# Last feed-forward stage: seven block products on token halves in place of eight

## What is computed

```python
D_FF_2 = -(-8 * D_MODEL // (3 * 256)) * 256          # 2816
...
h2 = modulate_2(x, shift2, scale2)                   # (1, 512, 1024)
y = (silu(h2 @ w_gate) * (h2 @ w_up)) @ w_down       # 2816 hidden columns
x = layer_norm(ALPHA * x + gate2 * y, ln2_g, ln2_b)
```

## Time and profile before

| | |
|---|---|
| median of 3 runs | 1970.53 us (1969.19 to 1971.74) |
| span of the profiled execution | 1965.3 us |
| median less span | 5.2 us |
| busy: PE, DVE, ACT, POOL | 97%, 60%, 40%, 17% of the span |
| last stage, first matmul to the norm's end | about 1582 to 1965 us |

### The profile page before, as it was taken

One profiled execution on the slowest core, in us unless ns is written; L12 is line 12 of the kernel. 1 busy time (PEld: TensorE's weight loads), 2 busy tenths in 40 slices (PEclk: granted clock), 3 DMA queues, 4 the chain that ended last, 5 costly groups with the idle time before them and its releaser, 6 DMA issues.

```text
span 1965.3 us, 22312 instructions
## 1 busy us (share of the span) xinstructions
PE 1906.1 (97%) x8952; PEld 1577.2 (80%) x8952; DVE 1180.5 (60%) x1853; ACT 779.4 (40%) x1180; POOL 343.6 (17%) x307
## 2 busy tenths in 40 slices
PE   4999999999999999999999999999999999999997
PEld 3788888878888887888788888877898778888886
DVE  6687665576676745665655644476777754433446
ACT  4677622352223235222422222256677442222223
POOL 4323111021111112002300000036533130000003
PEclk9999999999999999999999999999999999999998
DMA  9522366266566434432545432313211223223221
GB/s 333 150 84 70 134 223 237 88 226 221 217 209 219 150 107 158 164 127 86 213 173 192 173 127 86 108 65 129 70 44 65 88 85 100 93 90 103 95 99 43
DMA packets 126232, 267.54 MB, mean 136 GB/s; under 512 B 4576, under 2 KB 33264, under 8 KB 126129
## 3 DMA queue, kind: packets, MB, share of 16 engines
q1 hardware_dynamic: 121168, 248.59, 37.0%
q0 software_dynamic: 4960, 17.53, 2.5%
HBM read 261.84 MB, written 8.45 MB: 138 GB/s over the span
## 4 chain that ended last, share of the span: by engine, by line
PE 70%; DVE 3%; ACT 2%; POOL 2%; issue 1%; DVEq 0%; POOLq 0%; ACTq 0%
PE ps L624 22%; PE ps L626 22%; PE ps L625 22%; PE ps L784 1%; PE ps L773 0%; ACT t L1212 0%; PE ps L762 0%; ACT t L1216 0%; POOL t L2316 0%; PE ps L801 0%; PE ps L802 0%; PE ps L800 0%; DVE t L1628 0%; DVE t L1613 0%; POOL t L2125 0%
## 5 line engine op out<-in xcount | busy, mean ns | idle before, releaser
L624 PE MATMUL ps<-t 128*128 128x512 f32 (+1 forms) x2504 | 966.7, 386 | 10.3 <-POOL t L2220 4.2
L626 PE MATMUL ps<-t 128*128 128x512 f32 (+1 forms) x2504 | 958.9, 383 | 0.0
L625 PE MATMUL ps<-t 128*128 128x512 f32 (+1 forms) x2504 | 955.0, 381 | 0.0
L1549 DVE TENSOR_TENSOR t<-t 128x2048 fp32r<-128x2048 f32 x133 | 305.4, 2296 | 440.4 <-ACT t L1163 440.2
L624 PEld LDWEIGHTS ps<-t 128*128 128x128 f32 x2504 | 470.7, 188 | 104.5 <-POOL t L2125 5.6
L626 PEld LDWEIGHTS ps<-t 128*128 128x128 f32 x2504 | 470.3, 188 | 96.4
L625 PEld LDWEIGHTS ps<-t 128*128 128x128 f32 x2504 | 470.5, 188 | 90.8 <-issue 1.0
L1163 ACT ACTIVATE t<-t 128x2048 fp32r<-128x2048 f32 x133 | 254.3, 1912 | 612.8 <-PE ps L626 605.3
L1613 DVE SCALAR_TENSOR_TENSOR t<-ps,t 128x512 f32<-128x512 f32 x184 | 131.7, 748 | 81.4 <-PE ps L626 78.0
L1561 DVE CUSTOM_DVE_ANT_0 t<-t 128x1024 f32<-128x1024 f32 x144 | 174.8, 1255 | 6.7 <-DMA t<-in_adakv_t 3.5
L2125 POOL TENSOR_TENSOR t<-t 128x512 fp32r<-128x512 f32 x88 | 115.5, 1332 | 196.8 <-ACT t L1170 196.2
(11 more groups left out here) (171 smaller groups left out, 1526.1 us busy)
## 6 DMA issues: line engine op xcount, KB each, us to landing
t<-in_ada SPq DMA_DIRECT2D x48, 1024.0 KB, 5.9
t<-in_gate SPq DMA_DIRECT2D x22, 1024.0 KB, 5.1
t<-in_up SPq DMA_DIRECT2D x22, 1024.0 KB, 5.1
t<-in_down SPq DMA_DIRECT2D x22, 1024.0 KB, 5.0
t<-in_w_in SPq DMA_DIRECT2D x17, 1024.0 KB, 5.7
t<-in_w_mlp_in SPq DMA_DIRECT2D x16, 1024.0 KB, 5.3
t<-in_w_mlp_out SPq DMA_DIRECT2D x16, 1024.0 KB, 5.0
t<-in_ada_t POOLq DMA_DIRECT2D x13, 1024.0 KB, 6.0
```

The lines of the kernel that those rows point to most:

```text
L624: pe.matmul(o, wh, xh, start=first, stop=False)
L625: pe.matmul(o, wh, xl, start=False, stop=False)
L626: return pe.matmul(o, wl, xh, start=False, stop=last)
L1549: dve.tensor_tensor(WL[:, n % NW, :], raw[:, n % NRAW, :], WH[:, n % NW, :].bitcast(F), ALU.subtract).then_inc(w_lo_d.sem, w_lo_d.up("slot ...
```

## The change

Eighteen gate and up blocks of 1024 rows by 256 columns (shape "S", like B) are multiplied by a form of Strassen's scheme. The block is cut in quarters (row halves, column halves of 128), the input in quarters (feature halves, token halves of 256). Seven products of a quarter or a sum of quarters with an input quarter or a sum of them replace the eight; each is 4 `mm3` with 256 token columns, 12 matmuls, 84 in a block in place of 48 with 512 columns. The plain form stays for chunk 0 (gate and up) and for all of down.

The sums of weight quarters are made by POOL (`weight_sums`, four instructions a block, into the `csb` buffers), split by ACT (`sums_hi`) and DVE (`sums_lo`) into `SS`. Of the raw weights only three quarters are split (`raw_hi`, `raw_lo`). The four sums of input quarters are made and split once, during chunk 0, into `TT`, from an unsplit copy of the input `h6_all` that the norm before now keeps whole. The products lie in half banks of PSUM; ACT copies the first one out, DVE joins them in four steps (`first` to `fourth`). Then Silu (`silu`), the product with the gate (`times_gate`) and the split of the hidden tile (`hidden_hi`, `hidden_lo`) work on 1024 elements at once. The hidden tile has one buffer in place of two. A raw buffer is loaded again only when POOL has summed it too. Down of chunk 5 now goes "k" in its first half, as the other chunks did before.

```diff
-plan_ffn2(1)
...
+def plan_last():
+
+    for f in range(4):
+        for w, what in (("gate1", "gate"), ("up1", "up")):
+            for p in range(2):
+                if f:
+                    plan_role("S", w, 0, 512 * f + 256 * p, what, f, p)
+                else:
+                    plan_role("A", w, 512 * p, 0, what, f, p)
+        for hf in range(2):
+            plan_role("A", "down1", 512 * f, 512 * hf, "down", f, hf)
+    plan_role("S", "gate1", 0, 2560, "gate", 4, 0)
+    plan_role("S", "up1", 0, 2560, "up", 4, 0)
+    plan_role("S", "gate1", 0, 2048, "gate", 5, 0)
+    plan_role("C", "down1", 2560, 0, "down4", 4, 0)
+    plan_role("S", "gate1", 0, 2304, "gate", 5, 1)
+    for p in range(2):
+        plan_role("S", "up1", 0, 2048 + 256 * p, "up", 5, p)
+    for hf in range(2):
+        plan_role("A", "down1", 2048, 512 * hf, "down", 5, hf)
...
+            def seven_products(w, c0, before_last=None):
+                n = take("S", w, 0, c0)
+                b = bank_set(n)
+                hi, lo = slot_view(WH, n), slot_view(WL, n)
+                tops = [(HH[0][:, k, 0:256], HH[1][:, k, 0:256]) for k in range(KT)]
+                ends_ = [(HH[0][:, k, 256:512], HH[1][:, k, 256:512]) for k in range(KT)]
+                turned = [[(TT[:, 0, i, k, :], TT[:, 1, i, k, :]) for k in range(4)] for i in range(4)]
+                plain = [[(hi[:, k, blocks[m]], lo[:, k, blocks[m]]) for k in range(KT)] for m in range(2)]
+                sums = [[(SS[:, 0, i, blocks[k]], SS[:, 1, i, blocks[k]]) for k in range(4)] for i in range(4)]
+
+                def product(at, weights, inputs, name):
+                    o = region(b, at)
+                    for k in range(4):
+                        (wh, wl), (xh, xl) = weights[k], inputs[k]
+                        ins = mm3(o, wh, wl, xh, xl, k == 0, k == 3)
+                    ins.then_inc(mm.sem, mm.up("product", n, name))
+
+                on.wait_ge(w_lo_d, "raw", n, 0)
+                claim(4 * b)
+                product(0, plain[0][0:4], tops[0:4], 1)
+                product(1, plain[0][4:8], tops[4:8], 2)
+                on.wait_ge(w_lo_d, "raw", n, 1)
+                on.wait_ge(d_turn, "lo", 3)
+                claim(4 * b + 1)
+                product(3, plain[1][4:8], turned[3], 4)
+                mm.also("raw used", n)
+                on.wait_ge(d_sums, "pair", n, 0)
+                claim(4 * b + 2)
+                product(5, sums[0], turned[0], 5)
+                product(2, sums[1], turned[1], 6)
+                if before_last:
+                    before_last()
+                on.wait_ge(d_sums, "pair", n, 1)
+                product(4, sums[2], turned[2], 7)
+                claim(4 * b + 3)
+                product(6, sums[3], ends_[4:8], 3)
+                mm.also("slot", n)
+                freed[4 * b] = [(d_join, ("first", n))]
+                freed[4 * b + 1] = freed[4 * b + 2] = [(d_join, ("third", n))]
+                freed[4 * b + 3] = [(d_join, ("fourth", n))]
...
+                    for w in ("gate1", "up1"):
+                        for p in range(2):
+                            seven_products(w, 512 * f + 256 * p)
+                    down(f, "ki")
+                seven_products("gate1", 2560)
+                seven_products("up1", 2560)
+                seven_products("gate1", 2048)
...
+                def raw_hi(n, part):
+                    on.wait_ge(raw_in[n % NRAW], "landed", n)
+                    on.wait_ge(mm, "raw used" if in_products(n - NW) else "slot", n - NW)
+                    act.activation(raw_part(WH, n, part), raw_part(raw, n, part), ACT.Copy).then_inc(
+                        w_hi.sem, w_hi.up("raw", n, part))
+                def sums_hi(n, pair):
+                    on.wait_ge(p_sums, "pair", n, pair)
+                    if BEFORE[n] is None:
+                        on.wait_ge(d_turn, "lo", 3)
+                    else:
+                        on.wait_ge(mm, "product", BEFORE[n], (6, 3)[pair])
+                    act.activation(sum_pair(0, pair), csb[pair][:, :], ACT.Copy).then_inc(
+                        a_sums.sem, a_sums.up("pair", n, pair))
...
+                def hidden_hi(n):
+                    f, p = ROLE[n][1:]
+                    on.wait_ge(d_evac, "times", n)
+                    on.wait_ge(mm, "used", "act2", 1, f - 1)
+                    act.activation(AC7[:, 0, 2 * p:2 * p + 2, :].rearrange("p a n -> p (a n)"), joined(n), ACT.Copy).then_inc(
+                        a_hi.sem, a_hi.up("act2", 1, f, p))
...
+                def raw_lo(n, part):
+                    on.wait_ge(w_hi, "raw", n, part)
+                    dve.tensor_tensor(raw_part(WL, n, part), raw_part(raw, n, part), raw_part(WH, n, part).bitcast(F),
+                                      ALU.subtract).then_inc(w_lo_d.sem, w_lo_d.up("raw", n, part))
+                    if part:
+                        w_lo_d.also("slot", n)
+
+                def sums_lo(n, pair):
+                    on.wait_ge(a_sums, "pair", n, pair)
+                    dve.tensor_tensor(sum_pair(1, pair), csb[pair][:, :], sum_pair(0, pair).bitcast(F), ALU.subtract).then_inc(
+                        d_sums.sem, d_sums.up("pair", n, pair))
+
+                def first(n):
+                    on.wait_ge(a_evac, "first product", n)
+                    on.wait_ge(mm, "product", n, 6)
+                    f, p = ROLE[n][1:]
+                    if ROLE[n][0] == "up" and f > 1:
+                        on.wait_ge(a_hi, "act2", 1, *((f - 1, p) if (f, p) != (5, 1) else (3, 1)))
+                    elif ROLE[n][0] == "up":
+                        on.wait_ge(a_hi, "act2", 1, 0, 2 * p + 1)
+                    dve.tensor_tensor(joined(n)[:, 0:512].rearrange("p (a n) -> p a n", a=2), doubled(p1_b[:, :]),
+                                      two_regions(bank_set(n), 1, 2), ALU.add).then_inc(d_join.sem, d_join.up("first", n))
+
+                def second(n):
+                    on.wait_ge(mm, "product", n, 7)
+                    on.wait_ge(d_join, "first", n)
+                    dve.tensor_tensor(u34_b[:, :].rearrange("p (a n) -> p a n", a=2), doubled(joined(n)[:, 256:512]),
+                                      two_regions(bank_set(n), 4, 5), ALU.add).then_inc(d_join.sem, d_join.up("second", n))
+
+                def third(n):
+                    on.wait_ge(d_join, "second", n)
+                    dve.tensor_tensor(joined(n)[:, 512:1024].rearrange("p (a n) -> p a n", a=2), doubled(u34_b[:, 0:256]),
+                                      two_regions(bank_set(n), 3, 5), ALU.add).then_inc(d_join.sem, d_join.up("third", n))
+
+                def fourth(n):
+                    on.wait_ge(mm, "product", n, 3)
+                    dve.tensor_tensor(joined(n)[:, 256:512], u34_b[:, 256:512], region(bank_set(n), 6), ALU.add).then_inc(
+                        d_join.sem, d_join.up("fourth", n))
+                def times_gate(n):
+                    f, p = ROLE[n][1:]
+                    on.wait_ge(d_join, "fourth", n)
+                    on.wait_ge(a_evac, "silu", n - (1 if f == 4 else 2 if f < 4 or p else 3))
+                    dve.tensor_tensor(joined(n), joined(n), g7_b[:, p, :], ALU.mult).then_inc(
+                        d_evac.sem, d_evac.up("times", n))
+
+                def hidden_lo(n):
+                    f, p = ROLE[n][1:]
+                    on.wait_ge(a_hi, "act2", 1, f, p)
+                    dve.tensor_tensor(AC7[:, 1, 2 * p:2 * p + 2, :].rearrange("p a n -> p (a n)"), joined(n),
+                                      AC7[:, 0, 2 * p:2 * p + 2, :].rearrange("p a n -> p (a n)").bitcast(F),
+                                      ALU.subtract).then_inc(d_lo.sem, d_lo.up("act2", 1, f, 2 * p))
+                    d_lo.also("act2", 1, f, 2 * p + 1)
...
+            def weight_sums(n):
+                a21, a22, a11, a12 = (raw_block(raw, n, kq, m) for kq, m in ((0, 1), (1, 1), (0, 0), (1, 0)))
+                s = [sum_f(i).rearrange("p (k n) -> p k n", k=4) for i in range(4)]
+                on.wait_ge(raw_in[n % NRAW], "landed", n)
+                if BEFORE[n] is None:
+                    on.wait_ge(d_ada, "sum", len(ADA) - 1)
+                else:
+                    on.wait_ge(d_sums, "pair", BEFORE[n], 0)
+                pool.tensor_tensor(s[0], a21, a22, ALU.add).then_inc(p_sums.sem, p_sums.up("sum", n, 0))
+                on.wait_ge(p_sums, "sum", n, 0)
+                pool.tensor_tensor(s[1], s[0], a11, ALU.subtract).then_inc(p_sums.sem, p_sums.up("pair", n, 0))
+                if BEFORE[n] is not None:
+                    on.wait_ge(d_sums, "pair", BEFORE[n], 1)
+                pool.tensor_tensor(s[2], a11, a21, ALU.subtract).then_inc(p_sums.sem, p_sums.up("sum", n, 2))
+                on.wait_ge(p_sums, "pair", n, 0)
+                pool.tensor_tensor(s[3], a12, s[1], ALU.subtract).then_inc(p_sums.sem, p_sums.up("pair", n, 1))
...
+                    if in_products(n - NRAW):
```

(1 more changed line is left out.)

247 lines of the change are left out of this document (237 added, 10 removed).

## The result

The changed kernel took 1953.35 us (median of 4 runs, 1950.68 to 1956.02), the kernel before beside it on the same chip 1969.86 us (4 runs, 1969.11 to 1971.74). The ratio is 0.9917 with a 95% interval of 0.9904 to 0.993: faster by 0.8%. Forecast were 1954.7 us and a range of 1952 to 1961.

The account below looks back on a forecast made before the run. TensorE, busy 110.00 of 110 us in the last feed-forward stage, bounds the kernel. Eighteen blocks win 15.5 us and the chunk 5 entry 0.3; the 1965.3 us span becomes 1949.5, plus 5.2 gives 1954.7, range 1952 to 1961.

Parts of the forecast that it names:

- The pace of TensorE: Gate and up blocks: 84 matmuls of 256 columns take 10.07 us against 10.93, 0.86 us won a block.
- the rate of pairs does not hold: Rival: over 336 weight load and matmul pairs, each takes over 0.1301 us; at 0.14 the kernel takes 1985 us; chance 0.05.
- POOL's four sums set the pace: Rival: POOL's weight sums take more than 2.7 us each and lengthen blocks; at 3.3 about 1995 us; chance 0.03.
- The sum: Whole kernel: 15.5 us from eighteen blocks plus 0.3 at the chunk 5 entry, 15.8 us won.
- The 0.3 us of before goes: Entry of chunk 5's down: the old wait for a hidden low half, costing some 0.3 us, disappears.
- Down entries of chunks 1 to 3: After the last up block, DVE's hidden low half ends at 4.4 us, wanted at 5.47; slack 1.1, no wait.
- The term for POOL: A POOL sum ahead of the hidden low half at three down entries could cost 0 to 0.8 us; taken as 0.
- DVE and POOL exclude each other: Rival: the two engines' work stands end to end and TensorE waits; 8 us lost, 1962, or half, 1958; chance 0.12.
- The signs: Profile after: 256-column matmuls 0.120 us apart, DVE near 70% of a group, POOL sums of 1.3 to 1.6 us.
- One sign of being wrong: In the profile after, DVE's 1024-element low halves taking over 2 us beside POOL would show the prediction wrong.
- The fixed part of a matmul: TensorE: 0.1199 us at 256 columns against 0.2278 at 512 decides the gain, as instructions grow from 48 to 84.
- Room behind DVE: Chains of the sums in a block: slack of 4.5 us for pair 0 and 3.5 us for pair 1.

Follow-up runs that it names:

- two runs on the pairs of buffers: Changed kernel with products 5, 6 and 7 reading plain input quarters, 1950.32 us; changed kernel with the last product reading input sums, 1955.64 us.
- halved kernel: Kernel before, with 648 of the 512-column matmuls in 18 gate and up slots each issued as two of 256 columns; 1979.80 us, ratio 1.0031 to 1.0065.

## Why the prediction was right

- **The pace of TensorE**: forecast 10.07 us a block from 96 matmuls of the attention stage at 0.1199, measured 9.985. Products 1, 2, 5, 6 and 7 keep 0.12; product 4 (1.41) and product 3 (1.38) are the missing 0.085. The two runs on the pairs of buffers show where most of it comes from. The halved kernel shows 0.1199 over 90 matmuls again. The rival "the rate of pairs does not hold" is out: 336 in a row, four blocks, at 0.1189. So is "POOL's four sums set the pace": they take at most 2.10 us on average, under the 2.7 at which they would.
- **The sum**: forecast 15.8 us, measured 16.3 in the stage. That the two lie so close is in part luck, since three terms are off and partly cancel. The block is 0.085 us cheaper than forecast, 1.5 us more in 18 blocks. The slots that the blocks replace took 10.89 and not 10.93 (the rows of chunk 1 above), 0.6 us less: 18 x (10.89 - 9.985) = 16.3, the whole gain. And the entry of chunk 5, counted with 0.3 us won, lost a little (next point).
- **"The 0.3 us of before goes" (entry of f = 5)** was the step that failed, by some 0.5 us. The two down slots of chunk 5 took 22.44 us before (1925.50 to 1947.94) and take 22.60 now (1909.03 to 1931.63), where two others take 21.99 and 21.97. The wait moved and did not go. There DVE has 28 us of work in the 29 us ahead of the entry; the conversion of the down slot ran to 1908.9, the first join started only then, and the low half ended at 1914.98, 5.95 us after the slot's start, where 5.5 were allowed:

```profile
1913.76 1.22 DVE L2413 TENSOR_TENSOR t<-t 128x1024 fp32r<-128x1024 f32 x1 [1.13 <-ACT t L1739]
```

I had computed the entry from the last block alone, with an empty DVE ahead of it. Of the 28 us, 7.2 are the eight subtractions of the norm's shift (line 2441, between 1883.14 and 1899.06), which stand in no sum of the prediction, though the kernel before has them too. That POOL's lengthening was part of it is shown: without POOL the wait is gone.
- **Down entries of chunks 1 to 3**: forecast 4.4 us and no wait, measured 4.2 and no wait. The term for POOL, taken as 0, held because DVE's low half came first all three times, once by 0.36 us (the rows at 1756.38 above). Nothing in the schedule secures that order.
- **DVE and POOL exclude each other** (rival, 0.12): right in kind and wrong in its price, since what is late is not waited for. The Trainium skill ("SBUF — State Buffer", Who interferes with whom) has the same pair of operations interfering; the trace agrees for those that read two inputs from SBUF (0.69 to 1.49 us on average), and the joins with one input in PSUM kept 0.69.
- **The signs**: the spacing was 0.1189 us for 0.120. DVE was busy 76% of a group for the 70% forecast, and POOL's sums averaged 1.4 to 2.1 us for 1.3 to 1.6. One sign of being wrong did come, low halves of 1024 elements over 2 us: eight of 36 took 2.30. The time held all the same: TensorE waited once in the stage, 0.3 us, with one of the eight (at 1890.42) some way ahead of that wait.
- **The fixed part of a matmul**: the rows gave 0.012 us for splitting a 512-column matmul in two, and with it the gain of 15.5. By the formula of the Trainium skill ("TensorE: Matmul & The Clock Gate", Back-to-back issue gap) it would have been 21 us. The prediction left out that the section gives the formula for a matmul by itself and says that it is too low at few columns where each matmul comes with a weight load, as all do here. The stage shows 16.3, so the rows were the right source; at 128 columns the run shows 0.1116 us a matmul.
- **Room behind DVE** was claimed as 3.5 and 4.5 us for the chains of the sums. It is under 2.4 us a block when the work repeats, and about one in the run with nine matmuls fewer. This did not touch the forecast, but an estimate of a further step from these slacks would have failed.

## What to carry to other kernels

Price a matmul by one of the same shape in the same kernel: halving the columns costs 0.012 to 0.016 us for each matmul added, and so a scheme that drops an eighth of the columns brought 8 to 9% of the time of a block and not 12.5%, and at 128 columns a large loss (18.75 us a block). Take slacks over a whole period of the schedule, with the lengthened prices of operations that run beside each other, not chain by chain from an empty engine. The longer waits of TensorE here, 1.90 to 4.43 us, cost 1.4 to 1.9 times their length, since the clock was at its lower level behind them.
